# Neighbourhood attention in a hybrid encoder kernel: GpSimd divides the probabilities, the vector engine takes half of the copies of the transposed ones

## What is computed

```python
def neighborhood_attention(q, k, v, rpb):
    ...
    qb = q.reshape(B, H, rows, n_cb, Q_BLOCK_W, dh)
    kg = k[:, :, tok]
    vg = v[:, :, tok]
    s = jnp.einsum('bhrnqd,bhrnkd->bhrnqk', qb, kg).astype(jnp.float32) * (dh ** -0.5)
    bias = rpb.astype(jnp.float32)[:, ri, ci]
    s = jnp.where(mask[None, None, None], s + bias[None], NEG)
    p = jax.nn.softmax(s, axis=-1)
    o = jnp.einsum('bhrnqk,bhrnkd->bhrnqd', p.astype(v.dtype), vg)
```

## Time and profile before

| quantity | value |
|---|---|
| median of 3 runs | 1920.21 us (1917.53 to 1922.11) |
| the profiled execution's own time | 1914.64 us |
| its span, first to last instruction | 1912.9 us |
| busy: PE, DVE, ACT, POOL | 1604.2, 938.7, 316.4, 287.9 us |
| the stage in layer 1, first maximum to first matmul of the output projection | 297.38 to 335.73 us |
| the same stage in layer 2 | 1229.91 to 1267.91 us |

### The profile page before, as it was taken

How to read it: one execution, slowest core, us unless ns; L and a number is a source line. 1 busy time by engine, 2 the same in 40 slices (tenths; PEclk the granted TensorE clock), 3 DMA queues, 4 the chain that set the end, 5 groups by cost and what they waited for, 6 DMA issues and landing times.

```text
span 1912.9 us, 30047 instructions
## 1 busy us (share of the span) xinstructions
PE 1604.2 (84%) x9976; PEld 968.9 (51%) x9976; DVE 938.7 (49%) x1863; ACT 316.4 (17%) x666; POOL 287.9 (15%) x396
## 2 busy tenths in 40 slices
PE   2899997958997878997759999889498799998873
PEld 1375545845554445554425654478354455554441
DVE  3866856263442334343368585734543343443324
ACT  2243426100000000000032333431000000000000
POOL 0013221000121111211100140400111111111110
PEclk9999998978999999999979999999699999999997
DMA  8951441555999999899488317242589999999994
GB/s 260 312 183 49 142 141 47 231 214 204 399 411 407 405 411 403 345 412 405 187 270 279 94 45 219 90 193 112 223 336 405 406 396 403 402 412 409 408 394 198
DMA packets 150932, 538.61 MB, mean 282 GB/s; under 512 B 16942, under 2 KB 109342, under 8 KB 117566
## 3 DMA queue, kind: packets, MB, share of 16 engines
q1 hardware_dynamic: 135440, 514.17, 69.8%
q0 software_dynamic: 11520, 16.82, 2.7%
q10 hardware_dynamic: 3888, 6.61, 1.0%
HBM read 533.34 MB, written 25.20 MB: 292 GB/s over the span
## 4 chain that ended last, share of the span: by engine, by line
PE 47%; DMA 32%; DVE 7%; issue 6%; SPq 5%; ACT 2%; DVEq 0%; POOLq 0%; POOL 0%; ACTq 0%
PE bank L590 44%; DMA ring<-w 17%; DMA pool_b<-w 7%; DMA y_rows<-pool_a,row_now 2%; DMA pool_a<-xn_rows,tok_now 2%; PE bank L896 2%; DMA pool_b<-b_ada 2%; DVE low L1302 1%; SPq L455 1%; DMA pool_a<-y_rows 1%; PE bank L918 1%; ACT pool_a L1181 1%; SPq L439 1%; DVE ring L1480 1%; SPq L440 1%
## 5 line engine op out<-in xcount | busy, mean ns | idle before, releaser
L590 PE MATMUL bank<-ring,pool_a 128*64 128x256 f32 (+2 forms) x3968 | 553.7, 441 | 113.5 <-DMA ring<-w 70.2
L590 PEld LDWEIGHTS bank<-ring,pool_a 128*64 128x64 f32 (+1 forms) x3968 | 292.3, 142 | 353.2 <-issue 190.3
L1771 DVE TENSOR_SCALAR pool_a<-pool_a 128x256 f32<-128x256 f32 x72 | 21.2, 294 | 588.0 <-ACT pool_a L1213 588.0
L590 PE MATMUL bank<-hT,ring 128*128 128x512 f32 (+1 forms) x672 | 299.0, 601 | 3.7 <-DVE hT L1353 3.3
L590 PEld LDWEIGHTS bank<-hT,ring 128*128 128x128 f32 (+1 forms) x672 | 124.7, 188 | 161.0 <-issue 154.5
L1213 ACT ACTIVATE pool_a<-bank 128x256 f32<-128x256 f32 x72 | 27.6, 383 | 1021.8 <-PE bank L590 1021.8
L590 PE MATMUL bank<-ring,hT 128*128 128x256 f32 x768 | 170.6, 381 | 1.7 <-issue 1.7
L590 PEld LDWEIGHTS bank<-ring,hT 128*128 128x128 f32 x768 | 144.2, 190 | 24.9 <-issue 6.2
L1772 DVE RECIPROCAL pool_a<-pool_a 128x256 f32<-128x256 f32 x72 | 126.2, 1753 | 2.5
L1884 POOL DMA_INDIRECT pool_a<-xn_rows,tok_now x72 | 75.0, 1041 | 299.8 <-issue 122.7
L1784 DVE TENSOR_TENSOR pool_a<-bank,g_bc 64x512 f32<-64x512 f32 x144 | 99.2, 689 | 40.4 <-PE bank L590 32.2
(11 more groups left out here) (279 smaller groups left out, 1548.8 us busy)
## 6 DMA issues: line engine op xcount, KB each, us to landing
ring<-w SPq DMA_DIRECT2D x129, 2048.0 KB, 25.7
pool_b<-w SPq DMA_DIRECT2D x22, 2048.0 KB, 26.4
hT<-w SPq DMA_DIRECT2D x22, 2048.0 KB, 20.8
low<-w SPq DMA_DIRECT2D x22, 2048.0 KB, 22.9
ring<-w_ada SPq DMA_DIRECT2D x40, 1024.0 KB, 12.2
ring<-w_in SPq DMA_DIRECT2D x24, 1024.0 KB, 5.9
pool_b<-w_ada SPq DMA_DIRECT2D x16, 1024.0 KB
ring<-w_out SPq DMA_DIRECT2D x8, 1024.0 KB, 8.9
```

The lines of the kernel that those rows point to most:

```text
L590: return nc.tensor.matmul(out, lhsT, rhs, start=start, stop=stop, skip_group_check=True)
L1771: own(V.tensor_scalar(e1, e1, 1.0, None, ALU.add), t, 2)
```

## The change

The division of the probabilities goes from VectorE to GpSimd, which does it in four `tensor_scalar` instructions a head, for heads 0 and 1 behind the `bm` of heads 6 and 7, for the others in a loop behind that. VectorE only takes the reciprocals (`rsm_done`). The second of the two copies of the transposed probabilities of a head goes from ScalarE to VectorE, behind the reciprocals of head h-1; VectorE's loop gets one turn more for it. Both engines now wait for the product of the pair that last used the buffer (`on_done`), and the plan and the order of VectorE's takings are set to match. The number of VectorE's counted steps falls from 275 to 267.

```diff
@@ tile_plan
-            t += [(("PT", 2 * d - 2 + r, i), "a") for r in range(2) for i in range(2)]
+            t += [(("PT", 2 * d - 2 + r, i), "ad"[i]) for r in range(2) for i in range(2)]
@@ taken_at
+        if key[0] == "PT" and key[2] == 1 and key[1] < 6:
+            return index[("S", key[1] + 2, 1)] + 0.3
@@ tensor
-                        pe.wait_ge(act_took.s, act_took.at(l, taken[("PT", 2 * d + 1, 1)][1]))
+                        pe.wait_ge(act_took.s, act_took.at(l, taken[("PT", 2 * d + 1, 0)][1]))
+                        pe.wait_ge(dve_took.s, dve_took.at(l, taken[("PT", 2 * d + 1, 1)][1]))
@@ scalar
-                        for i in range(2):
-                            b = tile(("PT", g, i))
-                            F(PT_sb[:, g % 2, 2 * i:2 * i + 2, :].rearrange("p c n -> p (c n)"), b[:, :], ACT.Copy
-                              ).then_inc(act_took.s, 1)
+                        b = tile(("PT", g, 0))
+                        if g >= 2:
+                            act.wait_ge(on_done.s, on_done.at(l, g // 2))
+                        F(PT_sb[:, g % 2, 0:2, :].rearrange("p c n -> p (c n)"), b[:, :], ACT.Copy
+                          ).then_inc(act_took.s, 1)
@@ vector
-                for h in range(9):
+                for h in range(10):
...
-                    if h >= 1:
+                    if 1 <= h < 9:
                         g = h - 1
                         dve.wait_ge(sexp_done.s, sexp_done.at(l, g + 1))
-                        step(V.reciprocal(rsm[:, g % 2, :], sm[:, g % 2, :]))
-                        for cb in range(4):
-                            last = V.tensor_scalar(P_sb[:, g % 4, cb, :], P_sb[:, g % 4, cb, :],
-                                                   rsm[:, g % 2, cb:cb + 1], None, ALU.mult)
-                        last.then_inc(prob_done.s, 1)
+                        if g >= 2:
+                            dve.wait_ge(prob_done.s, prob_done.at(l, g - 1))
+                        V.reciprocal(rsm[:, g % 2, :], sm[:, g % 2, :]).then_inc(rsm_done.s, 1)
+                    if h >= 2:
+                        g = h - 2
+                        b = tile(("PT", g, 1))
+                        if g >= 2:
+                            dve.wait_ge(on_done.s, on_done.at(l, g // 2))
+                        V.tensor_copy(PT_sb[:, g % 2, 2:4, :].rearrange("p c n -> p (c n)"), b[:, :]
+                                      ).then_inc(dve_took.s, 1)
@@ gpsimd
+                def normalise(g):
+
+                    pool.wait_ge(rsm_done.s, rsm_done.at(l, g + 1))
+                    pass_on(pool)
+                    for cb in range(4):
+                        last = G_.tensor_scalar(P_sb[:, g % 4, cb, :], P_sb[:, g % 4, cb, :],
+                                                rsm[:, g % 2, cb:cb + 1], None, ALU.mult)
+                    last.then_inc(prob_done.s, 1)
+
                 for h in range(8):
...
                     last.then_inc(bm_done.s, 1)
+                    if h >= 6:
+                        normalise(h - 6)
+                for g in range(2, 8):
+                    normalise(g)
```

More of the change, by code:

```diff
@@ L60 @@
 WIN_PIECES = 12
-DVE_STEPS, ACT_STEPS = 275, 26
+DVE_STEPS, ACT_STEPS = 267, 26
 class Signal:
@@ L336, in build @@
         smax_done, sexp_done = sig("smax_done", 8), sig("sexp_done", 8)
-        prob_done = sig("prob_done", 8)
+        prob_done, rsm_done = sig("prob_done", 8), sig("rsm_done", 8)
         on_done = sig("on_done", 4)
```

## The result

The changed kernel takes **1936.52 us** (median of 4 runs, 1935.58 to 1941.75), the kernel before 1920.70 us on the same chip (4 runs). The ratio is 1.009, with a 95% interval from 1.0068 to 1.0112: **slower**, by 13 to 22 us. The forecast was 1921.2 us with a range to 1928.5 and called the two kernels the same, so it was wrong in size and in side.

A forecast was written before the change was run, and what follows sets the result against it. The prediction took a chain of waits across VectorE, TensorE and ScalarE in the stage before the output projection as the bound; +0.5 us a layer, +1.0 in two, gave a median of 1921.2 us, range 1916.5 to 1928.5.

The forecast's parts named there:

- d: Time from one GpSimd division instruction (128 x 256) to the next, four a head: 0.40 us, so 1.6 us a head.
- First part: Stage to 313 us: transposes of head 1 start at 303.9 + 8d = 307.1, before 307.13; change 0.0.
- New order on VectorE: Copies before maxima from head 3 on: exponential 5 +0.7 us, product 1 +0.25, exponential 7 +1.6.
- Third part: Stage's end, a chain from head 5's copies to output projection: product 2 +1.1 us, product 3 +0.5, leg between 4.7.
- rival 3: TensorE's clock falls a second time, before product 2: 2.7 us a layer, +6.4 in all, 1926.6 us; chance 0.06.
- second lateness: Above d = 0.65 GpSimd is late again, divisions 6 and 7 one behind the other, and sixteen times d count.
- rival 1: GpSimd pays per element as with two inputs, d = 0.73: +3.8 us a layer, +7.6 in all, 1927.8 us; chance 0.20.
- Contention: VectorE and GpSimd stopping each other in the stage: taken as 0, at the other end +1.6 us a layer.
- What costs nothing: Waits for `on_done` and, with d under 0.6, `prob_done`, VectorE's router-weight preparation and later weight transfers: no cost.
- unnamed losses: Losses outside the listed cases, given a chance of 0.02 and counted under slower.
- Rival 2: Clock does not fall in the first part, TensorE's gap being shorter: -4.4 us in all, 1915.8 us; chance 0.07.
- Rival 4: VectorE's order costs nothing, TensorE reaching the transposes earlier: stage 1 us shorter a layer, 1918.2 us; chance 0.04.

The follow-up runs named there:

- late_copy: Kernel before, VectorE still dividing, takes half of the copies, each one head later, behind the next maximum; 1922.19 us, ratio 1.0018.
- half_fill: Changed kernel, GpSimd dividing only two of four column blocks a head, with three matmuls nobody reads before product 2; 1920.42 us, ratio 1.0009.
- copy_only: Kernel before with only the second copy of each head moved to VectorE, which still divides; 1923.74 us, ratio 1.0011.
- probe: Kernel before with rows of single GpSimd instructions of one kind each added at its start, to time them; 1924.86 us in one execution.
- bm_wait: Kernel before, with GpSimd building the last two `bm` only when the maximum of head 3 is done; 1916.95 us, ratio 0.9988.
- after_fill2: Changed kernel with unread matmuls, 4 before the transposes of heads 0 and 1, 2 before heads 3 and 5, 1 before product 2; 1933.96 us.

## Why the prediction was wrong

**What bounds the kernel.** Right: the stage is a chain, and the total follows it. The stages lost 17.7 us and the median 15.8.

**GpSimd's price: the step that failed.** The forecast took d = 0.40 us from a range of 0.28 to 0.73; it is 0.90 in the stage and 0.91 alone. Two choices were wrong. The upper bound took it that a single input costs no more than two, which is false for these operations (0.91 against 0.69). And the value was put next to the one-input row, whose 0.28 us is another operation, on half the width. A memset's slope of 0.83 ns a column says nothing of an operation that takes 2.5. The Trainium skill (GPSIMD Engine Reference, section Engine selection) puts GpSimd at roughly line rate with one input. Here the measurement decides against that: 0.91 us, where VectorE does the same in 0.28 (1.14 for four). The forecast's -1.4 us beside that page would need a d of 0.25, below its own range, whose lower end of 0.28 gives -0.9.

**First part.** The formula was right, 303.9 + 8d: with 0.90 and this execution's start 1.54 us later it gives 312.64, and the transposes of head 1 stood at 312.74. So the term of 0.0 was mis-sized by 8 x 0.5 = 4.0 us, all of it from d. Measured: +4.07, counted from the stage's start.

**New order on VectorE.** Right: the copies alone cost +0.84 and +0.73 a layer at full clock for a forecast of +0.7, and late_copy showed the copy in front of the maximum as the cause in layer 1. With division at 1.82 us a head exponential 7 and product 2 were 0.3 and 0.5 us behind the forecast, and 0.4 of that is 4 x 0.91 against 8 x 0.40 in the first part.

**Third part, and the clock: the second step that failed.** The leg from product 2 to product 3 was forecast at 4.7 us and is 4.65 at full clock (half_fill). In the changed kernel it is 7.32 us, with product and transposes at half clock (3.68 and 2.85 us). That is rival 3, which had a chance of 0.06 and a price of 2.7 us a layer. The argument against it was a gap shorter than the 3.34 us in which the clock had stayed up, in one execution. The gap was shorter, 1.73 us in the changed kernel and 2.99 in copy_only, and the clock fell in both. In the kernels without fillers that divide on GpSimd or copy on VectorE it fell before product 2 in 12 layers of 12. With the order of the kernel before (that kernel, probe and bm_wait) it fell in 2 of 6. So it fell more often with the change, and the forecast had read one execution as a rule. What decides is open. It is not the gap's length, and not the run of 16 transposes ahead of it, which stood there in probe, bm_wait and late_copy too.

**The sum with the right price.** The forecast's own sensitivities, 8d to 0.65 and 16d above, give for d = 0.90: 0.5 + 8 x 0.25 + 16 x 0.25 = +6.5 a layer, 1933.2 us for the median. Measured are +8.8 and +8.9 in the stages and 1936.5 us. The legs of layer 1 show where the remaining 2.3 us come in; after_fill2 is the same kernel without the falls:

| starts behind the first maximum | before | forecast's formula, d = 0.90 | changed | after_fill2 |
|---|---|---|---|---|
| transposes of head 1 | 9.75 | 13.75 | 13.82 | 13.79 |
| product 0 | 15.30 | 19.30 | 19.10 | 16.74 |
| product 1 | 23.06 | 27.31 | 29.02 | 24.91 |
| product 2 | 30.27 | 35.37 | 37.13 | 32.93 |
| product 3 | 35.55 | 42.05 | 44.45 | 39.67 |

Between products 0 and 1 the changed kernel loses 1.7 us more than after_fill2, and its S tiles of heads 6 and 7, at half clock, take 3.68 us and not 2.00. This fall behind the wait for head 3's division stood in no rival. The last leg is 6.74 us in after_fill2 even at full clock, because the transposes of head 7 wait 1.88 us for GpSimd. That is the forecast's second lateness (divisions 6 and 7 one behind the other), 4.7 + 8 x 0.25 = 6.7. In the changed kernel the half clock hides this wait, so rival 3 added only 0.6 us to it. Of the 8.8 us, then, 0.5 are the forecast's, about 6 are the price of GpSimd's instruction, and about 2.3 are the two falls. The mechanism of rival 1 came true with a price outside its bounds, and that of rival 3 with it.

**Contention.** Right at 0. VectorE's negated maximum is 0.70 us once, at head 1, beside the `bm`, and 0.17 to 0.20 elsewhere, also where GpSimd divides; the copy that stands at 308.99 beside GpSimd's division is 0.69 us, as alone. The Trainium skill's rule (SBUF — State Buffer, section Who interferes with whom), that VectorE in a two-port mode and GpSimd exclude each other for the whole instruction, agrees: the four multiplications take 1.14 us by themselves and 3.16 beside the `bm`, and neither maxima nor copies out of PSUM are held.

**What costs nothing.** Right for the waits for `on_done` and `prob_done`: no copy and no reciprocal of the changed kernel is late for them, even at d = 0.90, above the 0.6 up to which the forecast called the second of them free.

**The chances.** The 0.02 of unnamed losses were counted with "the same" and not with "slower": the listed cases add up to 0.65 and 0.27, where the forecast has 0.67 and 0.25.

**Rivals 2 and 4.** Rival 2 (the first fall does not come) rested on transposes of head 0 coming earlier; they came later, behind 4.30 us of waiting. Rival 4 was not seen: product 1 does stand in front of the transposes.

## What to carry to other kernels

Before work goes to an engine whose price for this very operation, operand form and width is in no trace, measure that one instruction; a neighbour of another operation bounds it neither from below nor from above. If the work stands between two pieces of TensorE's work, price it twice: once as time on the chain, and once as what the clock may do behind the longer wait: here the falls that came with it made about 2.3 of 8.8 us. One execution in which the clock stays up through a gap is no proof that it will in the next. Idle TensorE time before a product can be filled with matmuls that nobody reads, if the fill is shorter than the wait by its measured length; one that was longer cost as much as the clock had.

## What the hardware showed that I had not expected

- On GpSimd, `tensor_scalar` 128 x 256 in f32 with a value per partition takes 0.91 us, `tensor_tensor` 0.69, `tensor_tensor` with a repeated value 0.58, a copy 0.36. One `tensor_tensor` over 128 x 1024 with the repeated reciprocals does in 1.89 us what four `tensor_scalar` did in 3.62.
- The granted clock fell ahead of product 2 behind idle stretches of 1.73 us (changed kernel), 2.47 (late_copy), 2.99 (copy_only), 3.34 (bm_wait, layer 2) and 3.35 (probe, layer 1, the code of the kernel before), and not behind 3.34 us before and in layer 1 of bm_wait. In late_copy, bm_wait and probe 16 transposes in one run stood ahead. So neither the length of the gap nor this run decides it, and one program does both. What does decide is open.
- GpSimd's lock follows the place: with `bm` built later, the division held for 2.66 us was free at 1.14, and another was held for 3.16.
